# A two-layer decoder trunk on one core: the input comes transposed and in pieces, the mixer's early work is reordered, the last output tile is made in two column halves

## The reference

```python
def rms_norm(x, g):
    y = xf * rsqrt(mean(xf * xf, axis=-1) + EPS);  return y * g
# layer 0
h = rms_norm(x, norm_mix_g[0])
q, k, v = split(h @ w_qkv, 3)
q = rope(rms_norm(q per head, q_gain), pos);  k = rope(rms_norm(k per head, k_gain), pos)
x = x + softmax(causal(q @ k.T * Dh ** -0.5)) @ v @ w_o
x = x + square(relu(rms_norm(x, norm_mlp_g[0]) @ w1)) @ w2
# layer 1: the same with retention(h @ w_in) @ w_out as the mixer, then the second MLP
```

## Time and profile before

| | us |
|---|---|
| three runs, median (lowest, highest) | 679.89 (679.13, 680.36) |
| the profiled execution, and its span | 680.12, 678.3 |
| PE busy in that span | 661.8 (98%) |
| DVE, ACT, POOL busy | 421.1, 330.1, 28.9 |

### The profile page before, as it was taken

The page is one execution under the profiler, slowest core; times in us unless marked ns, Lnnn a source line. Parts: engine busy times, 40 slices in busy tenths (PEclk is TensorE's granted clock), DMA queues, the critical chain, the costliest instruction groups (busy, mean ns, idle before and its releaser), DMA issues.

```text
span 678.3 us, 8852 instructions
## 1 busy us (share of the span) xinstructions
PE 661.8 (98%) x3293; PEld 558.2 (82%) x3293; DVE 421.1 (62%) x454; ACT 330.1 (49%) x423; POOL 28.9 (4%) x39
## 2 busy tenths in 40 slices
PE   2999999999999999999999999999999999999998
PEld 2888888888888888888888888888888888888886
DVE  2878675687777444557985556554468777744440
ACT  3866773655555333436445554543365555533320
POOL 3051200000000000000000000000000000000000
PEclk9999999999999999999999999999999999999999
DMA  8974337486655565563656535536648665555600
GB/s 292 334 244 131 128 120 236 129 242 186 186 186 188 198 202 194 189 202 129 189 187 190 180 124 186 186 125 186 191 120 246 189 186 186 186 187 196 205 1 31
DMA packets 81469, 121.93 MB, mean 180 GB/s; under 512 B 2032, under 2 KB 43152, under 8 KB 81440
## 3 DMA queue, kind: packets, MB, share of 16 engines
q1 hardware_dynamic: 80736, 119.55, 54.7%
q0 software_dynamic: 496, 1.90, 1.0%
q10 hardware_dynamic: 208, 0.08, 0.0%
HBM read 120.47 MB, written 1.05 MB: 179 GB/s over the span
## 4 chain that ended last, share of the span: by engine, by line
PE 95%; DMA 2%; DVE 2%; ACT 1%; SPq 0%; issue 0%; DVEq 0%; ACTq 0%
PE acc L473 22%; PE acc L433 19%; PE acc L435 19%; PE acc L434 19%; PE acc L476 11%; DMA x<-in_x 2%; PE scr L489 1%; DVE lo L880 1%; ACT hi L664 1%; PE scr L517 1%; PE scr L609 1%; PE scr L528 1%; PE scr L549 1%; PE scr L621 1%; DVE h_both L889 0%; PE scr L433 0%
## 5 line engine op out<-in xcount | busy, mean ns | idle before, releaser
L880 DVE TENSOR_TENSOR lo<-raw,hi 128x2048 fp32r<-128x2048 f32 x112 | 256.4, 2290 | 129.0 <-ACT hi L664 128.9
L664 ACT ACTIVATE hi<-raw 128x2048 fp32r<-128x2048 f32 x112 | 214.5, 1916 | 129.8 <-PE acc L435 129.8
L473 PE MATMUL acc<-h_both,hi 128*128 128x512 f32 x640 | 223.1, 395 | 0.0
L476 PE MATMUL acc<-h_both,lo 128*128 128x256 f32 x640 | 177.8, 278 | 0.0
L473 PEld LDWEIGHTS acc<-h_both,hi 128*128 128x128 f32 x640 | 120.1, 188 | 28.2
L476 PEld LDWEIGHTS acc<-h_both,lo 128*128 128x128 f32 x640 | 120.3, 188 | 0.0
L433 PE MATMUL acc<-hi,aT_hi 128*128 128x512 f32 x256 | 99.7, 389 | 0.0
L435 PE MATMUL acc<-hi,aT_lo 128*128 128x512 f32 x256 | 99.6, 389 | 0.0
L434 PE MATMUL acc<-lo,aT_hi 128*128 128x512 f32 x256 | 99.6, 389 | 0.0
L433 PE MATMUL acc<-hi,h_both 128*128 128x512 f32 x224 | 90.7, 405 | 0.0
L435 PE MATMUL acc<-hi,h_both 128*128 128x512 f32 x224 | 87.9, 393 | 0.0
(11 more groups left out here) (114 smaller groups left out, 530.8 us busy)
## 6 DMA issues: line engine op xcount, KB each, us to landing
raw<-in_mlp_w SPq DMA_DIRECT2D x64, 1024.0 KB, 5.4
raw<-in_r_w_in SPq DMA_DIRECT2D x24, 1024.0 KB, 5.1
raw<-in_a_w_qkv SPq DMA_DIRECT2D x12, 1024.0 KB, 5.7
raw<-in_r_w_out SPq DMA_DIRECT2D x8, 1024.0 KB, 5.0
raw<-in_a_w_o SPq DMA_DIRECT2D x4, 1024.0 KB, 5.0
x<-in_x SPq DMA_DIRECT2D x2, 512.0 KB, 11.5
out_x<-x SPq DMA_DIRECT2D x4, 256.0 KB, 3.9
decay_sb<-in_decay POOLq DMA_DIRECT2D x1, 768.0 KB, 5.3
```

Source lines behind the costliest of these rows:

```text
L473: nc.tensor.matmul(bank, feat_view(hi, s)[:, kt, o * P:(o + 1) * P], h_both[:, kt, :, :].rearrange("p b t -> p (b t)"), start=kt == 0, sto ...
L476: m = nc.tensor.matmul(bank[:, 0:SEQ], feat_view(lo, s)[:, kt, o * P:(o + 1) * P], hT_hi[:, kt, :], start=False, stop=kt == KD - 1)
L664: nc.scalar.activation(hi[:, s, :], raw[:, s, :], ACT.Copy).then_inc(hi_ready, 1)
L880: nc.vector.tensor_tensor(lo[:, s, :], raw[:, s, :], hi[:, s, :].bitcast(F32), ALU.subtract).then_inc(lo_ready, 1)
```

## The change

- The host lays out `xT` (x transposed) and one table `consts` with the identity and all gains in columns. PE's transposes of x and gains at the beginning, and ACT's copy, are gone. `xT` comes in four pieces of 1, 1, 2 and 4 row blocks; the first from ACT's queue, the others from SP between the quarters of chunk 0.
- Chunks 0, 1 and 2 are loaded, split and waited for in quarters (`load_parts`, `part_hi`, `part_lo`).
- POOL issues no transfer at the beginning. The rotary tables and head gains come in one transfer on SP behind chunk 2, x (for the norm's squares and the residual) behind chunk 6, then the mask; `rope_r` comes on POOL with `decay`, late.
- PE runs four matmuls on zeros while it waits, ACT loads its table then.
- The norm's squares move into slot 7, its variance into slot 8; `var` of the key tiles 2 and 3 comes before that of 0 and 1 (`VAR_ORDER`), and DVE waits for both scaled key tiles (`keys`, slot 9) before it goes on with `low` of chunk 7. `left` frees the accumulator apart from `var`. `low` of chunk 3 and of chunk 4 stand behind `rope` 0 and `rope` 1.
- The last chunk's second token tile is made in two halves of 256 columns in banks of their own and added to x after the earlier chunks' part; each half is written out by itself.

```diff
+    at[KEYS_AT].append(("keys", 0))
+    at[SCALES_AT].append(("scales", 0))
+    first = ["T", "factors", "square", "high", "var", "keys", "rope", "low", "raw", "left"]
...
+VAR_AT = [9, 9, 8, 9, 12, 13, 16, 17]
+VAR_ORDER = [2, 3, 0, 1, 4, 5, 6, 7]
+SQUARE_AT = 7
+FACTORS_AT = 8
+KEYS_AT = 9
+SCALES_AT = 14
-LOW_AT = {17: 18}
+LOW_AT = {1: 3, 3: 4, 17: 18}
+EARLY = 10
+XT_PIECES = [range(0, 1), range(1, 2), range(2, 4), range(4, KD)]
+PARTS = 3
...
-            load_qkv(0)
-            for n in range(2):
-                sp.dma_start(x[:, :, n * NC:(n + 1) * NC],
-                             xv[:, :, n * NC:(n + 1) * NC]).then_inc(x_in_ready[n], 16)
-            for c in range(1, 12):
+            load_parts(0, [0])
+            load_xT(1)
+            load_parts(0, [1])
+            load_xT(2)
+            load_parts(0, [2, 3])
+            load_xT(3)
+            load_parts(1)
+            load_parts(2)
+            sp.dma_start(rope_in[:], rope_a).then_inc(tables_in, 16)
+            for c in range(3, 7):
+                load_qkv(c)
+            sp.dma_start(x[:], xv).then_inc(x_in_ready, 16)
+            sp.dma_start(mask[:], causal).then_inc(mask_in, 16)
+            for c in range(7, 12):
                 load_qkv(c)
...
+            def last_chunk(c_g, s, k0, lhs):
+                chunk_in(c_g, s)
+                for kt in range(4):
+                    m = three(acc[:, 2, :], lhs[0][:, k0 + kt, 0:P], lhs[1][:, k0 + kt, 0:P],
+                              tok_view(hi, s)[:, kt, :], tok_view(lo, s)[:, kt, :], False, kt == 3)
+                m.then_inc(tok0_ready, 1)
+                for q in range(2):
+                    columns = slice(q * SEQ, (q + 1) * SEQ)
+                    for kt in range(4):
+                        m = three(scr[:, q, 0:SEQ], lhs[0][:, k0 + kt, P:SEQ], lhs[1][:, k0 + kt, P:SEQ],
+                                  tok_view(hi, s)[:, kt, columns], tok_view(lo, s)[:, kt, columns],
+                                  kt == 0, kt == 3)
+                    m.then_inc(last_columns_ready, 1)
...
-            pe.wait_ge(ident_in_sem, 16)
-            pe.wait_ge(gains_in, 32)
-            nc.tensor.transpose(acc[:, 0, 0:4 * KD], gain_rows[:],
-                                ident[0:4 * KD, 0:4 * KD]).then_inc(gainsT_ready, 1)
-            for n in range(2):
-                pe.wait_ge(x_in_ready[n], 16)
-                transpose_x(0, range(4 * n, 4 * n + 4))
+            pe.wait_ge(zeros_ready, 1)
+            for _ in range(4):
+                nc.tensor.matmul(acc[:, 3, 0:SEQ], sT[:, 0:P], sT[:, 0:SEQ], start=True, stop=True)
+            pe.wait_ge(consts_in, 16)
...
+            act.dma_start(consts[:], consts_src).then_inc(consts_in, 16)
+            act.dma_start(xT_in[:, 0:1, :], xT_src[:, 0:1, :]).then_inc(xT_in_ready[0], 16)
+            act.wait_ge(zeros_ready, 1)
+            nc.scalar.activation(junk[:, 0:1], sT[:, 0:1], ACT.Copy).then_inc(table_loaded, 1)
+            act.wait_ge(consts_in, 16)
+            first_hi(0)
+            part_hi(0, [0])
+            first_hi(1)
+            part_hi(0, [1])
+            first_hi(2)
+            part_hi(0, [2, 3])
+            first_hi(3)
+            part_hi(1)
+            part_hi(2)
...
+            for c in range(2):
+                for kt in range(4):
+                    first_lo([4 * c + kt])
+                    part_lo(c, [kt])
+            part_lo(2)
...
+                    elif what == "keys":
+                        dve.wait_ge(k_scaled, 2)
...
+            def last_update():
+                xs = x[:, 1, NC:2 * NC]
+                dve.wait_ge(used, C_W2[1] + 8 + 6 + 1 + RING)
+                own(nc.vector.scalar_tensor_tensor(xs, acc[:, 3, :], nrm[:, 2, 1:2], xs, ALU.mult, ALU.add))
+                update_x(3, 1, None, 2, TOK_W2[1] + 1, scale=2, tiles=[0])
+                for q in range(2):
+                    xq = x[:, 1, NC + q * SEQ:NC + (q + 1) * SEQ]
+                    dve.wait_ge(last_columns_ready, q + 1)
+                    nc.vector.scalar_tensor_tensor(xq, scr[:, q, 0:SEQ], nrm[:, 2, 1:2], xq, ALU.mult,
+                                                   ALU.add).then_inc(out_quarter_ready, 1)
```

More of the change, by code:

```diff
@@ L123, in attention_schedule @@
         at[O_AT[h]].append(("O", h))
-    early = ["N", "rope", "high", "low", "v", "raw", "var", "T", "A", "P", "S", "E"]
+    at[KEYS_AT].append(("keys", 0))
+    at[SCALES_AT].append(("scales", 0))
+    first = ["T", "factors", "square", "high", "var", "keys", "rope", "low", "raw", "left"]
+    early = ["N", "scales", "rope", "high", "low", "v", "raw", "left", "var", "T", "A", "P", "S", "E"]
     late = ["N", "A", "S", "v", "high", "O", "P", "E", "low"]
     for k in range(SLOTS):
-        first_to_last = early if k < LATE else late
-        at[k].sort(key=lambda what: (first_to_last.index(what[0]), what[1]))
-    return at
+        first_to_last = first if k < EARLY else early if k < LATE else late
+        at[k].sort(key=lambda what: (first_to_last.index(what[0]), VAR_ORDER.index(what[1]) if what[0] == "var"
+                                     else what[1]))
+    return at
+VAR_AT = [9, 9, 8, 9, 12, 13, 16, 17]
[4 more added lines that the diff above has]
+SCALES_AT = 14
 S_AT = [12, 13, 15, 17, 20, 21, 22, 23]
@@ L139 @@
 V_AT = [19, 20, 23, 23]
-LOW_AT = {17: 18}
+LOW_AT = {1: 3, 3: 4, 17: 18}
+EARLY = 10
 LATE = 20
 SCHEDULE = attention_schedule()
+SQUARES_BEFORE = sum(what == "raw" for k in range(SQUARE_AT) for what, _ in SCHEDULE[k])
+POWER_NO = [VAR_ORDER.index(p) + 2 if VAR_ORDER.index(p) >= 4 else VAR_ORDER.index(p) + 1 for p in range(8)]
+NORM_POWER_NO = 5
+XT_PIECES = [range(0, 1), range(1, 2), range(2, 4), range(4, KD)]
+PARTS = 3
 class Ticks:
@@ L392, in norm_power, with head_power @@
                 power(nrm[:, 1, :], nrm[:, 0, :], TT)
-            norm_power()
-            pool.wait_ge(pl.sem, pl.now())
-            pool.sem_inc(tables_g_ready, 1)
-            for p_i in range(8):
+            def head_power(p_i):
                 j, t = p_i // 2, p_i % 2
-                ss = small[:, 4 * t:4 * t + 4]
+                ss = head_sums[:, p_i, :]
                 if j % 2 == 0:
@@ L435, in three, with token_chunk @@
                 return nc.tensor.matmul(dst, a_lo, b_hi, start=False, stop=last)
-            def token_chunk(c_g, s, first, last, k0, bank0, slot, lhs, after=lambda t: None):
-                chunk_in(c_g, s)
+            def token_chunk(c_g, s, first, last, k0, bank0, slot, lhs, after=lambda t: None,
+                            close_second=False):
+                parts = isinstance(c_g, int) and c_g == 0 and s < PARTS
+                if not parts:
+                    chunk_in(c_g, s)
                 for t in range(TT):
@@ L447, in token_chunk @@
                                   tok_view(hi, s)[:, kt, :], tok_view(lo, s)[:, kt, :],
-                                  first and kt == 0, last and kt == 3)
+                                  first and kt == 0, (last or close_second and t == 1) and kt == 3)
                     if t == 0 and last:
@@ L1154, in _ @@
             mlp(1, 3)
+            last_update()
 def shape_tables():
@@ L1197 @@
     named = {k: np.ascontiguousarray(inputs[k]) for k in _INS}
-    for n, a in zip(("rope_a", "rope_r", "decay", "causal", "ident"), shape_tables()):
-        named[n] = a
+    rope_a, rope_r, decay, mask, ident = shape_tables()
+    rope_in, consts, xT = laid_out(rope_a, ident, *[np.asarray(inputs[k]) for k in (
+        "x", "norm_mix_g", "norm_mlp_g", "a_q_gain", "a_k_gain")])
+    tables = {"rope_in": rope_in, "rope_r": rope_r, "decay": decay, "causal": mask, "consts": consts,
+              "xT": xT}
+    named.update(tables)
     for n, a in named.items():
```

240 lines of the change are left out of this document (160 added, 80 removed).

## The result

The changed kernel takes 674.75 us (median of 4 runs, 673.71 to 677.14) against 679.79 us for the kernel before beside it: ratio 0.9935, 95% interval 0.992 to 0.9951. It is faster, as forecast; the forecast was 671.3, and its range ended at 674.5.

The account below looks back on a forecast made before the run. PE, busy 98% of the span, was taken as the bound. Start -11.3, lag +3.1 and end -0.35 sum to -8.55 us: 671.6 from the profiled 680.12, forecast 671.3 against the median of the runs, range 667.9 to 674.5.

Parts of the forecast that it names:

- What bounds it: Whole kernel: PE works 98% of the span, so a change pays only where PE stands still, starts late or ends late.
- E: Moment when the transposes of `T` 1, behind slot 7, end on PE; 41.03 us in the kernel before by the prediction.
- Landings: First transfers: small ones land after 2.0 us, then 387 KB per us; x^T there at 7.8 us, chunk 3 at 16.8.
- The term: Beginning: chunk 2 starts at 17.9 us instead of 29.2, a gain of 11.3 us (8.7 to 12.1).
- The clock: Beginning: PE's clock rises at about 8 to 9 us; some twelve matmuls cost 0.2 us more each.
- The lag: Slots 7 to 15: work moved onto ACT, DVE and POOL puts PE 3.1 us back by `T` 5 (0 to 4.5).
- The end: Last tile in column halves: shorter last addition and transfer, slightly more matmul time, sum -0.35 us (-0.5 to +0.1).
- 1, the lag doesn't reach PE: Slots 7 to 15: PE hides the moved work and loses nothing there; 668.2 us, chance 0.22.
- 2, the late start: Beginning: first x^T piece takes 4.9 us, clock rises after 11 us, chunk 1 ends at 20.5; 673.9 us, chance 0.16.
- 3, PE stays at 1.2 GHz: First three chunks: feeding in pieces keeps PE at the lower clock, 0.43 us per matmul; 684.1 us, chance 0.04.
- 4, x too late: Slot 8: x behind seven chunks lands so late that ACT stands at its squares; about 679.5 us, chance 0.03.
- The range: Whole time: 667.9 to 674.5 us, meant to hold 8 in 10 and take in most of rivals 1 and 2.

Follow-up runs that it names:

- the second execution: The changed kernel profiled again with no edit; the profiled execution took 674.30 us, the median of its runs was 674.78 us, ratio to the kernel before 0.9921.

## Why the prediction was wrong, step by step

- **What bounds it**: right. PE is the bound from E on, and only where it stood still was there anything to gain.
- **Landings: the step that failed.** "A small transfer issued into empty queues landed after 2.0 us ... After that the rate of 387 KB per us counts." Neither holds for a queue that is just filling. Whole x^T landed at 10.5 instead of 7.8, the piece before it at 7.9, chunk 3 at 19.6 instead of 16.8. I added one 2.0 us at the beginning, counted bytes at the rate of a window at 16 us, and let each transfer be there with its last byte. The third piece, by that count due at about 5.0 (an estimate: 1104 KB, of which 336 land at 3.0), landed at 7.9. The runs show two errors: the rate of the first 8 us is below 387 (1104 KB had been moved at 5.9), and a transfer lands with its slowest part, 1.4 to 2.0 us behind the in-order count. The kernel before had shown the first, in rows I did not read. Its windows of 7 to 10 us:
```profile
7.00:8.00 1.00, 0.28 (x1) 0.18 (x1) 0.00 (x0) 0.56 (x2) 0.00 (x0) 1.00 1.52 117
8.00:9.00 1.00, 0.00 (x0) 0.00 (x0) 0.00 (x0) 1.00 (x1) 0.00 (x0) 1.00 0.61 75
9.00:10.00 1.00, 0.00 (x0) 0.00 (x0) 0.53 (x1) 0.44 (x1) 0.00 (x0) 1.00 0.70 260
```
 and the second half of x landed 12.59 us after its issue, at 14.45. A count of the 2.1 MB up to it at 387 from 2.5 us on puts it at about 8, and with the 1.1 MB that POOL's transfers moved meanwhile at about 11.
- **The term**: E came 8.85 us earlier with one rise of the clock at 10.2, 6.84 with a fall at 8.4 that lasted until 15.2; the term said 11.3, with 8.7 as its worst bound, so that the first is barely inside and the second outside. The first pair was ready 1.85 us later than 5.2, but that alone is not it, as the run with the piece on SP shows: the third pair is the bound, ready at 10.2 where my intervals gave 7.2. From there 42 matmuls of the two chunks remain, at 0.227 each 9.5 us, with some 0.6 of short gaps: chunk 2 begins at about 20.3 where I had 17.9.
- **The clock**: the rise at 8 to 9 was nearly right (10.2). What I had not considered is that it can rise on the zeros, at 5.0, and be taken back at 8.4 after PE's idle time. The Trainium skill, "TensorE: Matmul & The Clock Gate", "HAM oscillation", describes a level that falls again and again where matmuls wait for transfers. This trace agrees in kind, though its longest wait ahead of the fall, 1.86 us, is shorter than those of the page's case. It makes two kinds of execution, 2 us apart, of one kernel.
- **The lag**: right in mechanism and nearly in size, 3.45 for 3.1, with the waits 0.84, 0.65 and 1.36 for 0.6, 0.9 and 1.6. From the prediction's own E the squares of x ended at 3.5 (forecast 3.4) and the key tiles were scaled at 10.2 (9.8); the 0.4 is less than the 0.78 that DVE's last step of `rope` 3 lost beside POOL, a collision I had looked for on POOL alone. Removing its two causes took away all but 0.3 of it, 2.0 and 1.1 us.
- **The end**: -0.35 forecast, -0.4 measured.
- **Rivals**: 1, the lag doesn't reach PE: false. 2, the late start: nearest to what happened, in time (673.9) and in kind. I had tied it to the place of the first piece in ACT's queue, which proved to decide nothing, and gave it 0.16. 3, PE stays at 1.2 GHz: not for three chunks, but from 8.4 to 15.2 it does in some executions, for 2 us and not 12. 4, x too late: x landed at 30.4, before the store of `T` 1 was done (34.8); false.
- **The range** was the bound of one landing (6.1 for 3.4) and took the rate as known. Had the rate of the early windows been in it, the term would have reached down to about 6.5 (an estimate: in the windows of the kernel before, the 2.1 MB up to the last piece of x^T have moved by 10.0, 2.2 us behind my 7.8, to be taken off the bound of 8.7).

In the sum of the second execution, the start is short of its term by 2.45 us, the lag over by 0.35, the end within 0.1: 671.6 + 2.45 + 0.35 gives 674.4, and it took 674.3.

## What to carry to other kernels

Count the arrivals of a kernel's first microseconds from the windows of those same microseconds, and let each transfer land with its slowest part (here 1.4 to 2.0 us behind the count in order); then look for the piece that the engine wants last, since bringing the first one forward moves nothing. A wait that spares a helper engine a collision must be weighed against what stands behind it on the waiting engine: here 1.95 us of an idle DVE became 2.0 us on PE, where the collision had cost 0.19. Work that has a free slot before the crowded stretch belongs there, but not at the price of moving its data ahead of weights in the queue.
